# A 1,024-wide two-block transformer on one core: another order of squaring and scaling in the first block's feed-forward

## The reference

```python
    x = x + jnp.concatenate([y_moba, y_mlstm, y_swa], axis=-1) @ w_out
    u = rms_norm(x, ln2) @ w_up
    return x + jnp.square(jax.nn.relu(u)) @ w_down
```

## Time and profile before

| | us |
|---|---|
| median of 3 runs | 1854.07 |
| lowest and highest of them | 1853.41, 1857.15 |
| profiled execution | 1858.29 |
| its span in the trace | 1856.5 |
| TensorE busy in it | 1768.7 (95%) |

### The profile page before, as it was taken

How to read it: one execution, slowest core, us unless ns; L and a number is a source line. 1 busy time by engine, 2 the same in 40 slices (tenths; PEclk the granted TensorE clock), 3 DMA queues, 4 the chain that set the end, 5 groups by cost and what they waited for, 6 DMA issues and landing times.

```text
span 1856.5 us, 25437 instructions
## 1 busy us (share of the span) xinstructions
PE 1768.7 (95%) x9838; PEld 1496.4 (81%) x9838; DVE 1281.6 (69%) x2083; ACT 997.8 (54%) x1672; POOL 113.4 (6%) x72
## 2 busy tenths in 40 slices
PE   7888989997999999999999989999999999989999
PEld 5767878885777788888787878888888887778888
DVE  5675666576466657876677767776787757677874
ACT  5564554456355545554457745545555445755552
POOL 0500000040000000000220000000000202000000
PEclk9988999997889999999999989999999999999999
DMA  7703456551254555555652235555555654045554
GB/s 268 216 1 137 170 170 216 204 193 46 71 199 174 194 201 182 195 182 205 228 180 91 94 137 201 182 204 184 198 186 204 227 181 159 27 156 181 183 203 137
DMA packets 62022, 313.97 MB, mean 169 GB/s; under 512 B 22685, under 2 KB 24353, under 8 KB 25294
## 3 DMA queue, kind: packets, MB, share of 16 engines
q1 hardware_dynamic: 60382, 303.93, 46.5%
q0 software_dynamic: 1232, 4.22, 0.8%
q10 hardware_dynamic: 288, 4.19, 0.6%
HBM read 311.25 MB, written 7.36 MB: 172 GB/s over the span
## 4 chain that ended last, share of the span: by engine, by line
PE 74%; DVE 12%; ACT 8%; issue 4%; SPq 1%; DMA 1%; ACTq 0%; DVEq 0%
PE acc L405 37%; PE acc L407 18%; DVE w_lo L380 6%; ACT w_hi L371 3%; PE acc L394 3%; PE acc L395 3%; PE acc L396 3%; PE tp L759 2%; DVE pre L568 1%; PE acc L787 1%; ACT sqh L1171 1%; DVE pre L1339 1%; PE acc L788 1%; PE sc L743 1%; PE acc L414 1%
## 5 line engine op out<-in xcount | busy, mean ns | idle before, releaser
L380 DVE TENSOR_TENSOR w_lo<-raw,w_hi 128x1024 fp32r<-128x1024 f32 (+1 forms) x564 | 692.4, 1235 | 350.8 <-ACT w_hi L371 349.1
L371 ACT ACTIVATE w_hi<-raw 128x1024 fp32r<-128x1024 f32 (+1 forms) x564 | 582.6, 1038 | 224.2 <-PE acc L407 117.8
L405 PE MATMUL acc<-act_a,w_hi 128*128 128x512 f32 x1552 | 550.1, 399 | 8.8 <-DVE w_lo L380 8.6
L407 PE MATMUL acc<-act_a,w_lo 128*128 128x256 f32 x1552 | 434.2, 280 | 0.0
L405 PE MATMUL acc<-hidden,w_hi 128*128 128x512 f32 x1216 | 425.4, 395 | 4.0 <-DVE w_lo L380 4.0
L405 PEld LDWEIGHTS acc<-act_a,w_hi 128*128 128x128 f32 x1552 | 293.5, 189 | 82.8 <-issue 14.0
L407 PE MATMUL acc<-hidden,w_lo 128*128 128x256 f32 x1216 | 339.8, 279 | 0.0
L407 PEld LDWEIGHTS acc<-act_a,w_lo 128*128 128x128 f32 x1552 | 294.3, 190 | 0.1
L405 PEld LDWEIGHTS acc<-hidden,w_hi 128*128 128x128 f32 x1216 | 228.0, 187 | 58.5 <-DVE w_lo L380 5.3
L405 PE MATMUL acc<-act_b,w_hi 128*128 128x512 f32 x688 | 245.4, 400 | 0.0
L562 ACT COPY part<-acc 128x256 f32<-128x256 f32 x272 | 100.4, 369 | 266.3 <-PE acc L407 265.3
(11 more groups left out here) (187 smaller groups left out, 2023.9 us busy)
## 6 DMA issues: line engine op xcount, KB each, us to landing
raw<-in_slabs SPq DMA_DIRECT2D x282, 1024.0 KB, 4.8
na_skew<-in_rpb SPq DMA_DIRECT2D x32, 128.0 KB
na_bias<-na_skew ACTq DMA_DIRECT2D x2, 2048.0 KB, 8.5
t_skew<-t_by_distance POOLq DMA_DIRECT2D x2, 1024.0 KB, 14.1
t_bias<-t_skew POOLq DMA_DIRECT2D x1, 2048.0 KB, 8.7
x_res<-in_x SPq DMA_DIRECT2D x1, 1024.0 KB, 5.1
out_x<-x_res SPq DMA_DIRECT2D x8, 128.0 KB, 5.1
prow<-in_prow SPq DMA_DIRECT2D x1, 518.0 KB
```

The costliest lines, as they stand in the source:

```text
L371: nc.scalar.activation(w_hi[u % RING][:, 0:n], raw[j % RAW][:, (u % 2) * HALF:(u % 2) * HALF + n], ACT.Copy).then_inc(s["unit_hi"], 1)
L380: nc.vector.tensor_tensor(w_lo[u % RING][:, 0:n], raw[j % RAW][:, (u % 2) * HALF:(u % 2) * HALF + n], w_hi[u % RING][:, 0:n].bitcast(F32), ...
L405: nc.tensor.matmul(bank[:, :], wh, src[:, c + i, :, :].rearrange("p i s -> p (i s)"), start=first and i == 0, stop=False, skip_group_check ...
L407: mm = nc.tensor.matmul(bank[:, S:2 * S], wl, src[:, c + i, 0, :], start=False, stop=last and i == n - 1, skip_group_check=True)
```

## The change

Two tables of places move: the sum over partitions stands after up unit 1 instead of 0, and the spreading of the result after unit 3 instead of 2 (RSUM1, BCAST1).

In the loop over m, both engines now make all eight chunks of `act_a` first and square and add all eight afterwards.

In the up projection, pre_of(p) moves from step 2p+3 to step 2p+1 of VectorE (pair 0, which needs `r_bc`, to step 3), ScalarE's squares of pair p from step 2p+3 to step 2p+2 (pairs 0 and 1 to steps 4 and 5), and low_of(p) from step 2p+4 to step 2p+3 (pairs 0 and 1 to steps 5 and 6). No instruction is added or removed.

```diff
+        RSUM1, BCAST1 = 1, 3
@@ pe_layer1, also in act_layer1 and dve_layer1
-                if n == 0:
+                if n == RSUM1:
                     pe_rsum(pe, b)
-                if n == 2:
+                if n == BCAST1:
                     pe_bcast(pe, b)
@@ act_layer1 (dve_layer1 with dve_square in the same way)
                 for n in (2 * m, 2 * m + 1):
                     act_chunk(act, b, act_a, gain, n)
-                for n in (2 * m, 2 * m + 1):
-                    act_square(act, b, n)
+            for n in range(DC):
+                act_square(act, b, n)
@@ act_layer1, the two activations stand in squares_of(p) now
-                if n >= 3 and n % 2 or n == FC1:
-                    p = (n - 3) // 2 if n < FC1 else FC1 // 2 - 1
+                if n >= 4 and n % 2 == 0:
+                    squares_of(n // 2 - 2 if n == 4 else n // 2 - 1)
+                if n == 5:
+                    squares_of(1)
+            squares_of(FC1 // 2 - 1)
@@ dve_layer1
-                    dve.wait_ge(s["hid_hi"], b.at("hid") + 1)
+                    dve.wait_ge(s["hid_hi"], hid0 + n // 2 - 1)
-                if n == 2:
+                if n == BCAST1:
                     dve_bcast(b)
+                    pre_of(0)
                 if n >= 3 and n % 2:
-                    pre_of((n - 3) // 2)
-                if n >= 4 and n % 2 == 0:
-                    low_of((n - 4) // 2)
-            pre_of(FC1 // 2 - 1)
-            low_of(FC1 // 2 - 2)
+                    pre_of(n // 2)
+                if n >= 5 and n % 2:
+                    low_of(0 if n == 5 else n // 2 - 1)
+                if n == 6:
+                    low_of(1)
             low_of(FC1 // 2 - 1)
```

More of the change, by code:

```diff
@@ L1149, in act_layer1, with squares_of @@
                     act_chunk(act, b, act_a, gain, n)
-                for n in (2 * m, 2 * m + 1):
-                    act_square(act, b, n)
+            for n in range(DC):
+                act_square(act, b, n)
             b.mark("tile_done", 2)
             layer_over(b, LAYER1)
[L1155 to L1160, removed]
+            def squares_of(p):
+                k = b.mark("hid")
+                act.wait_ge(s["pre_ready"], k)
+                nc.scalar.activation(h[:, 2 * p:2 * p + 2, 0, :], pre[p % 2][:, :, :], ACT.Square)
+                if p >= 2:
+                    act.wait_ge(s["hid_lo"], k - 2)
+                nc.scalar.activation(sqh[p % 2][:, :, :], pre[p % 2][:, :, :], ACT.Square)\
+                    .then_inc(s["hid_hi"], 1)
+            for n in range(FC1):
+                b.unit += 1
+                act_split(act, b, b.unit + RING - 1)
+                act_part(act, b)
+                if n == RSUM1:
                     act_ms(b)
-                if n == 2:
+                if n == BCAST1:
                     act_bcast(act, b)
-                if n >= 3 and n % 2 or n == FC1:
-                    k = b.mark("hid")
-                    p = (n - 3) // 2 if n < FC1 else FC1 // 2 - 1
[L1167 to L1172, removed]
+                if n >= 4 and n % 2 == 0:
[3 more added lines that the diff above has]
+            squares_of(FC1 // 2 - 1)
             act_down(act, b, DOWN1, act_a, next_gain)
@@ L1331, in dve_layer1 @@
                     dve_chunk(dve, b, act_a, gain, n)
-                for n in (2 * m, 2 * m + 1):
-                    dve_square(dve, b, n)
+            for n in range(DC):
+                dve_square(dve, b, n)
             layer_over(b, LAYER1)
@@ L1346, in low_of @@
                     .then_inc(s["hid_lo"], 1)
-            part0 = b.at("part")
+            part0, hid0 = b.at("part"), b.at("hid")
             for n in range(FC1):
@@ L1352, in dve_layer1 @@
                 if n >= 4 and n % 2 == 0:
-                    dve.wait_ge(s["hid_hi"], b.at("hid") + 1)
+                    dve.wait_ge(s["hid_hi"], hid0 + n // 2 - 1)
                 dve_sum(dve, b, pre[n // 2 % 2][:, n % 2, :])
-                if n == 0:
+                if n == RSUM1:
                     dve_ms(dve, b)
-                if n == 1:
+                if n == RSUM1 + 1:
                     dve_diag(dve, b)
-                if n == 2:
+                if n == BCAST1:
                     dve_bcast(b)
+                    pre_of(0)
                 if n >= 3 and n % 2:
-                    pre_of((n - 3) // 2)
-                if n >= 4 and n % 2 == 0:
-                    low_of((n - 4) // 2)
-            pre_of(FC1 // 2 - 1)
-            low_of(FC1 // 2 - 2)
+                    pre_of(n // 2)
[3 more added lines that the diff above has]
+                    low_of(1)
             low_of(FC1 // 2 - 1)
```

## The result

The changed kernel ran at 1832.26 us at the median of 4 (1827.35 to 1833.42), the kernel before beside it at 1855.61 (4 runs). The ratio on record, taken over all runs, is 0.9861 with a 95% interval of 0.9839 to 0.9884: faster by 21.5 to 29.9 us. The two medians alone are 23.35 apart (0.9874). 23.4 us and a time of 1830.7 had been forecast. The profiled execution took 1833.09, its span 1831.3, 25.2 less than the one before.

The account below looks back on a forecast made before the run. A loop of waits between VectorE and ScalarE was taken to bound the up projection. Its reordering (19.2 us) plus chunks first (4.2) gave 23.4, from 1854.07 to 1830.7 us, range 1825 to 1838.

Parts of the forecast that it names:

- The loop and its size: Up projection: VectorE and ScalarE wait on each other, 6.40 us per pair against TensorE's 5.55; 9.6 lost per layer.
- The new loop under TensorE's pitch: Up projection, reordered: the VectorE-ScalarE loop takes 4.32 us per pair, under TensorE's 5.55, giving back 9.6 per layer.
- The margin of 1.2: Up projection: the reordered loop of 4.32 us stays 1.2 per pair under TensorE's 5.55.
- Part 2, the chunks: Start of up projection: all chunks first, squares behind; the last chunk pair reaches TensorE 2.3 us earlier.
- The net gain of 2.1: Start of up projection: with the clock falling again, chunks first gains 1.5 to 2.7 us, taken as 2.1 per layer.
- the clock rival: Start of up projection: the clock does not fall, 4.2 us gained per layer instead of 2.1; 1826.5; chance 0.22.
- The sum: Whole kernel: 19.2 us from the up projection's order plus 4.2 from chunks first, 23.4 in all.
- Carrying the gain over to the median: Whole kernel: the profiled execution's gain taken unchanged from the median, 1854.07 - 23.4 = 1830.7 us.
- Partly bound: Up projection: VectorE misses slots, 5.97 us per pair, total gain 13.8, time 1840.3; chance 0.14.
- nothing gained: Up projection: squares only change places with the wait, VectorE idles as long elsewhere; 1854 us; chance 0.04.
- Slabs: Up projections: later low halves delay slab transfers; at a landing of 15 us, 6.67 per pair, 1861; chance 0.05.
- the loop of 6.40 per pair: Up projection before the change: start-to-start waits between VectorE and ScalarE total 6.40 us, 0.85 slower than TensorE per pair.

Follow-up runs that it names:

- e1: Kernel before with only the up projection's new order of scaling, squares and low part; chunk loop, sum and spreading as before; 1825.93 us, ratio 0.9829.
- e6: Kernel before with one more ScalarE activation per pair ahead of the two squares, result unchanged; 1871.88 us, ratio 1.0085.
- e7: Changed kernel with one more ScalarE activation per pair ahead of the two squares; 1830.12 us, ratio 0.9840 to the kernel before.
- e5: Changed kernel with ScalarE's squares moved back to step 2p+1, VectorE's low part to 2p+2; 1855.58 us, ratio 0.9991 to the kernel before.
- e3: Changed kernel with the first chunks' squares made and added between rounds of the loop over m; 1815.27 us, ratio 0.9775 to the kernel before.
- e4: Changed kernel run again without edits; 1825.60 us, ratio 0.9834 to the kernel before.
- e11: Changed kernel run a third time without edits; 1830.07 us, ratio 0.9857 to the kernel before.

## Why the prediction was right, step by step

**The loop and its size.** Right. The loss was forecast at 9.6 per layer, and e1 gave back 9.65. e6 shows that the chain of starts read from the earlier trace rows is the loop: 0.53 put in made it 0.52 longer.

**The new loop under TensorE's pitch.** Right, by the waits that are gone; its own length, 4.32, was some 0.18 too short, since a scaling right behind its own sum starts later (0.52 in the changed kernel). I had taken the 0.34 of a row where the scaling took an older pair. The margin of 1.2 covered it, and e7 puts another 0.53 in without loss.

**Part 2, the chunks.** The last chunk pair reached TensorE 9.68 us after the first addition to the residual, against 12.02 before: 2.34 earlier, 2.3 forecast. The net gain of 2.1 was right in size (111.3 - 109.15 = 2.15), but by luck, since it came by another course than either branch. I asked whether the clock falls between the chunk pairs or not at all. The forecast said that it falls there and that unit 1 runs at half clock. It did not fall there, unit 1 ran at full clock, unit 2 then waited 1.02 for its low half as the clock rival said, and behind that wait the clock fell. So the forecast's step for part 2 failed. The rival's failed too, because it had no price for its own gap: it gave unit 2 2.8 where it took 4.42, and it had the low half 0.4 too early, so its 4.2 became about 2. Where the clock did fall between the chunk pairs (e5, layer 2), it was back 3.4 us later and unit 4 began 3.8 earlier than before, not 2.1: in that branch the slow time was forecast too long.

**The sum.** 23.4 was forecast, the stretches give 22.0 in the first trace and 23.6 at the quick pitch; the first median difference is 23.35. A match to 0.1 is luck: the later sessions showed 31.2 and 27.6, and by the stretches the difference lies outside the edited stages. Carrying the gain over to the median was good only to some 4 us or worse, since the kernel before spread over 1848 to 1865 in all sessions, not over the 4 us of the three runs I had.

**The rivals.** Partly bound and nothing gained are excluded by e1 and e7. Slabs: in no trace did ScalarE wait for a slab in the middle of the up projections, where they landed at most 7.7 us after their issue. With TensorE at full pace they came in time.

## What to carry to other kernels

When two in-order engines hand work to each other and neither is busy, add the start-to-start times round the loop of waits, compare that with the pitch of the engine that should bound, and move the answer to a request at least one independent instruction behind the request; moving the request earlier alone (e5) changes nothing. Work taken out of a critical chain has to go somewhere: put it into waits that the chain has anyway (e3), not in one block behind it, where it delays the next thing and opens a gap behind which, here, the clock fell as well.

## What the runs showed of the hardware

**Two pitches of TensorE.** At full granted clock a pair of products (512 and 256 columns) takes 0.3466 or 0.3534 us, constant over tens to hundreds of us; in the stretches read here it changed only across a stop of TensorE. In the changed kernel's first trace units come at 2.83 in layer 1 (184.58 to 187.40 in the timeline) and at 2.77 in layer 2; in e4 it is the other way round (stretches 109.16 and 110.75), in e7 and e11 both are quick. So it is not set by the code. It is worth 1.6 us over one layer stretch. In the kernel before, TensorE ran at the quick pitch up to its first wait and mostly at the slower one between the short waits. That is some 0.7 us of product time in layer 1, but it need not have cost any: by the loop of 6.40 per pair, a quicker pitch would only have made the waits longer.

**The same attention code takes 48.8 to 58.4 us**, with a mean granted clock of 0.90 to 0.71. Two single executions of this kernel can differ by 10 us and more with the same code (the kernel before: 1848 to 1865), while a stretch between two landmarks repeats within 0.2 at equal pitch.
